# Two small constant loads issued by ScalarE instead of SyncE, in a two-block transformer kernel

## The chip, the cores and the metric

The kernel runs on 1 core of one Trainium2 chip. The metric is device time in microseconds (us): the median of several runs, and beside it one execution recorded by the hardware profiler. PE is TensorE's matmul, PEld its weight load, DVE is VectorE, ACT is ScalarE, POOL is GpSimd, SP is SyncE; "DMA" is the core's 16 transfer engines, which all work on each of the large transfers named here.

## The reference, cut to what matters

Two transformer blocks run one after the other on 512 tokens of width 1024, in float32. The first block is modulated by a conditioning vector `c`; only its first lines touch the place of the change:

```
c_act = silu(c)                                   # c is [1, 1024]
mod = c_act @ ada_w + ada_b                       # [1, 6*1024]: sh1, sc1, ga1, sh2, sc2, ga2
h = rmsnorm(x, pre_mix_g) * (1.0 + sc1) + sh1     # x is [512, 1024]
proj = h @ w_in                                   # convolution input (glu), q, k, v, gates
...
x = x + ga1 * rmsnorm(mixer(proj), post_mix_g)
x = x + ga2 * rmsnorm(swiglu_ffn(...), post_ffn_g)
x = second_block(x)                               # retention, MLA attention, convolutional FFN
```

So the first matrix product, `h @ w_in`, needs three things: the norm of `x`, the scale and shift `sc1` and `sh1` that come from `silu(c)` and 2 of the 6 parts of `ada_w`, and the weights.

## The kernel before, in words

Everything is stored transposed: 1024 features are 8 chunks of 128 partitions, and the 512 tokens lie along the free dimension. Each engine runs its own written-out program, one after another, and they meet at semaphores. Every float32 product is made of three products of split operands (`_hi` and `_lo`). Work goes in stages of weight groups (`STAGES`), and the first stage is `glu`, whose 8 chunks (`glu_chunk`, L761) each need one chunk of `h_hi` and `h_lo`.

The start of the program has four strands.

**Transfers.** SP issues all of them, from one queue, in the order in which its program is written: `small` (128 x 24 numbers, among them `c` as a column per chunk and the constant eps), `ident` (the 128 x 128 identity), four parts of `x` (512 KB each), `vec` (the vectors), two tiles of `ada_w` for chunk 0 (`load_first(0)`, L463, 512 KB each), half a weight group of glu (`glu_half(0)`, L468, 512 KB). Then SP waits until the fourth part of `x` is in, and goes on with further tiles of `ada_w` and of glu weights.

**The conditioning row.** ACT loads its function table (L1360), waits for `small` and takes exp(-c) (L1362). DVE makes `silu(c)` out of it in three tiny steps (L2308 to L2312), waits for `ident`, and spreads the 1024 values along diagonals (`c_spread`, L2315). PE multiplies that by a matrix of ones (L733), and so has the whole row of `silu(c)` on every partition, and DVE copies it out of PSUM into `c_row` (L2321). `c_columns`, the function with L2308 to L2315, is the first thing in DVE's program after two memsets, and the copy stands after the second of DVE's four `add_pair` steps:

```
c_columns()
for quarter in range(4):
    add_pair(quarter)
    if quarter == 1:
        c_copy()
dve.wait_ge(sem["in_vec"], 16)
dve.wait_ge(sem["c_act"], 8)
for c in range(DC):
    modulate(c)
```

**The norm.** ACT squares each part of `x` as it lands (L1366, `sq_first`), DVE adds pairs of chunks (`add_pair`, L2349), PE sums over partitions (L738), ACT takes the logarithm and the exponential (L1330, L1333) and so gets `rs`.

**The first chunk of h.** DVE multiplies a tile of `ada_w` by `c_row` and sums along it (`ada_column`, L2298), twice for a chunk: once for the scale, once for the shift. Then it makes `t_n` (L2274), and ACT adds the shift and rounds to `h_hi` (L1357), after it has rounded the first half of the weights to `w_hi` (L1372). PE's first matmul of the glu stage (L761) waits for both. Before that PE runs matmuls of a matrix of ones that nothing reads (L726, `warm`), and in its program the product with `c_spread` stands between the first 9 of them and the sums of L738.

Of the kernel before, what the change touches and what calls it, by code (L numbers as in the profile page):

```python
# [218 lines left out]
def build(nc, dram, out):  # L219
# [4 lines left out]
    def fixed(name, shape, dt=F32):  # L224
        size = int(np.prod(shape[1:])) * 4
        t = nc.alloc_sbuf_tensor_at(name, shape, dt, offset=off[0])
        off[0] += (size + 31) // 32 * 32
        return t
# [9 lines left out]
    vec, small = fixed("vec", [P, N_VEC]), fixed("small", [P, N_SMALL])  # L238
# [5 lines left out]
    ident, ones_r, block_mean = fixed("ident", [P, P]), fixed("ones", [P, P], F32R), fixed("block_mean", [P, P])  # L244
# [133 lines left out]
    with ExitStack() as ctx:  # L378
        sem = {n: ctx.enter_context(nc.semaphore(n)) for n in names}
# [67 lines left out]
        def _(sp):  # L447
# [25 lines left out]
                for r, buf in enumerate(bufs):  # L473
                    sp.dma_start(buf[:, :], dram["ada"][a + r]).then_inc(sem[done], 16)

            sp.dma_start(small[:, :], dram["small"]).then_inc(sem["in_small"], 16)
            sp.dma_start(ident[:, :], dram["mats"][:, 0, :]).then_inc(sem["in_ident"], 16)
            for part in range(4):
                two = slice(2 * part, 2 * part + 2)
                sp.dma_start(x[:, two, :], dram["x"][:, two, :]).then_inc(sem[f"x_ada{part}"], 16)  # L480
# [741 lines left out]
        def _(act):  # L1222
# [16 lines left out]
            def fold_highs(stage, k):  # L1239

                name, slot, n = stage.name, k % 2, fold_nth[stage.name, k]
                ext_hi, _, ext_f = fold_ext(stage)
                act.wait_ge(raw_full[slot], 16 * (stage.g0 // 2 + k // 2 + 1))
                again = k - 2 >= FOLDS[name]
                if again:
                    act.wait_ge(sem["fold_mm"], mm_count[name, k - 2, 2])
                else:
                    act.wait_ge(sem["tile_done"], 2 * (stage.g0 + k) - 2)
                yield A(block_of(w_hi[slot], LEFT), block_of(raw[slot], LEFT), ACT.Copy).then_inc(sem["fold_hi"], 1)
                act.wait_ge(sem["fold_sum"], 4 * n + 3)  # L1250
                if again:
                    act.wait_ge(sem["fold_mm"], mm_count[name, k - 2, 5])
                yield A(ext_hi[slot][:, :, :, :], ext_f[slot][:, :, :, :], ACT.Copy).then_inc(sem["fold_hi"], 1)
                act.wait_ge(sem["fold_sum"], 4 * n + 4)
                if again:
                    act.wait_ge(sem["tile_done"], 2 * (stage.g0 + k) - 2)
                yield A(block_of(w_hi[slot], RIGHT), block_of(raw[slot], RIGHT), ACT.Copy).then_inc(sem["w_hi_done"], 1)
# [99 lines left out]
                    A(dst, src[:, :], ACT.Identity, bias=shift).then_inc(sem["made_hi"], 1)  # L1357


            nc.scalar.preload_act_table_set("natural_log_exp_and_others")  # L1360
            act.wait_ge(sem["in_small"], 16)
            A(row_stat[:, 0, 0:DC], small[:, SMALL["c"]:SMALL["c"] + DC], ACT.Exp, scale=-1.0).then_inc(sem["c_act"], 1)  # L1362
# [565 lines left out]
            def ret_pair(stage, i0):  # L1928
                def evac(_, slot, k, ahead):
                    i = i0 + k  # L1930
                    for s in range(2):
                        n = 2 * i + s
                        if s == 1 and i < PAIRS - 1:
                            act.wait_ge(sem["z_done"], HEADS + n + 1)
                            stage_q(i + 1, rqk)
                        act.wait_ge(sem["sp_done"], 2 * HEADS + n + 1)
                        A(t_hi[:, :], rp[:, :], ACT.Copy).then_inc(sem["sph_done"], 1)
                        if s == 0:
                            ahead()
                        elif i < PAIRS - 1:  # L1940
                            stage_qk(i + 1, rqk, rkey_dup, begun=True)
                        if n < 4:
                            decays(n + 4)
                        else:
                            beside_scores(n)
                        act.wait_ge(sem["ro_done"], n + 1)
                        A(rqk[head_rows(s), i, :], o_ps[0:HD, :], ACT.Copy).then_inc(sem["o_half"], 1)
                        if n >= 4:
                            beside_values(n)
                    if i < PAIRS - 1:  # L1950
                        act.wait_ge(sem["v_centred"], max(1, i + 1))
                        stage_v(i + 1, rv_rows, ret_v)
                return evac
# [195 lines left out]
        def _(dve):  # L2149
# [836 lines left out]

            def ret_pair(i0):
                def evac(_, slot, k, ahead):
                    i = i0 + k
                    for s in range(2):  # L2990
# [518 lines left out]
```

## Time and profile before

| | |
|---|---|
| median of 3 runs | 1330.96 us (1330.03 to 1331.42) |
| the profiled execution, its own time | 1328.96 us |
| its span, first to last instruction | 1327.10 us |
| PE matmul busy | 1309.0 us (99% of the span) |
| DVE busy | 1045.7 us (79%) |
| ACT busy | 731.6 us (55%) |
| first matmul of the glu stage starts | 16.04 us |

The times of the engines come from the profiled execution, whose own time is 1.86 us longer than the span between its first and last instruction. It is 2.00 us below the median of the runs shown, and 1.07 us below the lowest of them. Busy shares are averages over all stages. The first 16 us, before the glu stage starts, are another regime than the rest.

### The profile page before, as it was taken

The page shows a single profiled execution, that of the slowest core. Times are in us where ns is not written, and L with a number is a line of the kernel's source. Part 1 is how long each engine was busy: PE and PEld are TensorE (multiplying, and loading weights), DVE is VectorE, ACT ScalarE, POOL GpSimd, SP SyncE. Part 2 cuts the span into 40 slices and gives each one's busy share as a digit, 9 for nine tenths or more (in the row PEclk, how much of TensorE's full clock was granted, in tenths as well). Part 3 has the DMA queues.
Part 4 walks back from the last instruction along what each step waited for, and adds up shares of the span by engine and source line. Part 5 has one row for each costly group of instructions (what it writes and reads, how often), then busy time and mean ns, then how long its engine had stood idle before and what let it go on. Part 6 is the DMA issues. An engine that isn't in the chain of part 4 may idle for free. (4 is left out here: it accounts for less than half of the span.)

```text
span 1327.1 us, 19480 instructions
## 1 busy us (share of the span) xinstructions
PE 1309.0 (99%) x7546; PEld 1150.7 (87%) x7546; DVE 1045.7 (79%) x1317; ACT 731.6 (55%) x1045; POOL 113.2 (9%) x86
## 2 busy tenths in 40 slices
PE   8999999999999999999999999999999999999997
PEld 6889888879989989989999897888888898889886
DVE  7899999999989689746849769997577876786663
ACT  4424888785546345534545856787365434443444
POOL 0000000012100591000012001010200000000001
PEclk9999999999999999999999999999999999999999
DMA  9634411167333433222252151301222232223212
GB/s 366 256 128 112 159 63 48 33 220 277 131 149 104 143 143 122 101 96 96 96 191 72 64 175 48 93 27 64 96 95 95 95 100 91 95 95 128 77 69 76
DMA packets 28731, 155.60 MB, mean 117 GB/s; under 512 B 3248, under 2 KB 5680, under 8 KB 15600
## 3 DMA queue, kind: packets, MB, share of 16 engines
q1 hardware_dynamic: 28656, 154.58, 33.4%
q8 instruction: 50, 0.82, 0.3%
q14 instruction: 25, 0.20, 0.0%
HBM read 145.39 MB, written 4.19 MB: 113 GB/s over the span
## 5 line engine op out<-in xcount | busy, mean ns | idle before, releaser
L2155 DVE TENSOR_TENSOR w_lo<-raw,w_hi 128x2048 fp32r<-128x2048 f32 (+3 forms) x139 | 249.4, 1796 | 47.0 <-ACT w_hi L1237 35.3
L1237 ACT ACTIVATE w_hi<-raw 128x2048 fp32r<-128x2048 f32 (+2 forms) x74 | 131.2, 1773 | 31.3 <-PE psum L920 15.4
L658 PE MATMUL psum<-h_hi,w_hi 128*128 128x512 f32 x360 | 92.1, 394 | 0.1
L658 PE MATMUL psum<-h_hi,w_lo 128*128 128x512 f32 x360 | 91.1, 391 | 0.0
L658 PE MATMUL psum<-h_lo,w_hi 128*128 128x512 f32 x360 | 90.4, 389 | 0.0
L658 PE MATMUL psum<-xg_hi,w_hi 128*128 128x512 f32 x336 | 83.0, 389 | 0.0
L658 PE MATMUL psum<-xg_hi,w_lo 128*128 128x512 f32 x336 | 83.0, 389 | 0.0
L658 PE MATMUL psum<-xg_lo,w_hi 128*128 128x512 f32 x336 | 83.0, 389 | 0.0
L658 PEld LDWEIGHTS psum<-h_lo,w_hi 128*128 128x128 f32 x360 | 67.6, 188 | 14.1
L658 PEld LDWEIGHTS psum<-h_hi,w_lo 128*128 128x128 f32 x360 | 67.0, 188 | 13.7
L658 PEld LDWEIGHTS psum<-h_hi,w_hi 128*128 128x128 f32 x360 | 66.0, 188 | 14.2 <-DVE w_lo L2155 0.7
L3220 DVE TENSOR_TENSOR up_raw<-psum,rs 128x512 f32<-128x512 f32 x44 | 30.2, 687 | 56.5 <-PE psum L658 54.2
L658 PEld LDWEIGHTS psum<-xg_lo,w_hi 128*128 128x128 f32 x336 | 63.1, 188 | 13.1
L658 PEld LDWEIGHTS psum<-xg_hi,w_lo 128*128 128x128 f32 x336 | 63.1, 188 | 13.1
L658 PEld LDWEIGHTS psum<-xg_hi,w_hi 128*128 128x128 f32 x336 | 62.9, 188 | 13.0
L3360 POOL COPY sq_sum<-sq 128x256 f32<-128x256 f32 (+1 forms) x6 | 3.6, 608 | 622.3 <-ACT sq L1323 622.3
L2091 ACT ACTIVATE up_a<-up_raw,vec 128x512 f32<-128x512 f32 x22 | 18.0, 816 | 58.5 <-DVE up_raw L3220 58.5
L2091 ACT ACTIVATE up_b<-up_raw,vec 128x512 f32<-128x512 f32 x22 | 17.9, 816 | 53.9 <-DVE up_raw L3220 53.9
L920 PE MATMUL psum<-h_hi,w_hi 128*128 128x256 f32 x288 | 46.5, 284 | 0.3 <-DVE act_p L2712 0.2
L2437 DVE SCALAR_TENSOR_TENSOR conv_tmp<-u,vec,conv_tmp 128x512 f32<-128x512 f32 x62 | 46.7, 753 | 0.0
L920 PE MATMUL psum<-h_lo,w_hi 128*128 128x256 f32 x288 | 46.3, 283 | 0.0
L920 PE MATMUL psum<-h_hi,w_lo 128*128 128x256 f32 x288 | 46.3, 283 | 0.0
(501 smaller groups left out, 3336.7 us busy)
## 6 DMA issues: line engine op xcount, KB each, us to landing
raw<-w_ffn_in SPq DMA_DIRECT2D x22, 1024.0 KB, 4.9
raw<-w_up SPq DMA_DIRECT2D x22, 1024.0 KB, 4.8
ada_first<-ada SPq DMA_DIRECT2D x16, 512.0 KB, 12.0
raw<-w_gate SPq DMA_DIRECT2D x8, 1024.0 KB, 4.9
raw<-w_mix_out SPq DMA_DIRECT2D x8, 1024.0 KB, 4.9
raw<-w_ffn_out SPq DMA_DIRECT2D x8, 1024.0 KB, 4.9
raw<-w_down SPq DMA_DIRECT2D x8, 1024.0 KB, 4.8
ada_x<-ada SPq DMA_DIRECT2D x11, 512.0 KB, 5.3
```

The lines of the kernel that those rows point to most:

```text
L658: last = mm(ps, w[slot][:, k, t * P:(t + 1) * P], part(xv, k0 + k), start=first, stop=final)
L920: last = mm(into, w[a][:, k, :], xv[b][:, k, :], start=(p in (1, 7) and a == b and k == 0), stop=(b == 1 and k == 3), skip_group_check=True)
L1237: A(w_hi[slot][:, 0:stage.kc, :], raw[slot][:, 0:stage.kc, :], ACT.Copy).then_inc(sem["w_hi_done"], 1)
L2091: A(buf[:, :], up_raw[t][s][:, :], ACT.Identity, scale=col("conv_w_2", 2 * 2 * FC + t * FC + chan), bias=col("conv_b_2", t * FC + chan)).t ...
L2155: return tt(out_lo, full, high.bitcast(F32), ALU.subtract)
L2437: stt(u[:, c, PAD:PAD + S] if last else sums[a][:, :], u[:, c, bass.ds(j, S)], col("conv_w", c * TAPS + j), sums[a][:, :], ALU.mult, ALU.a ...
L3220: by_rs = lambda: tt(up_raw[t][s][:, :], bank[2 * s + t], rs[:, :], ALU.mult)
L3360: last = nc.gpsimd.tensor_copy(sq_sum[:, cols], sq[q % 2][:, cols])
```

## The change

The transfers of `small` and `ident` leave SP's program, where they were its first two, and become the first two things that ACT issues, ahead of the load of its function table. Neither what is moved nor who waits for it is changed. All names and line numbers in the text are those of the kernel before, except in rows that are marked as the changed kernel's.

```diff
@@ block.sync
-            sp.dma_start(small[:, :], dram["small"]).then_inc(sem["in_small"], 16)
-            sp.dma_start(ident[:, :], dram["mats"][:, 0, :]).then_inc(sem["in_ident"], 16)
             for part in range(4):
                 two = slice(2 * part, 2 * part + 2)
                 sp.dma_start(x[:, two, :], dram["x"][:, two, :]).then_inc(sem[f"x_ada{part}"], 16)
@@ block.scalar
+            act.dma_start(small[:, :], dram["small"]).then_inc(sem["in_small"], 16)
+            act.dma_start(ident[:, :], dram["mats"][:, 0, :]).then_inc(sem["in_ident"], 16)
             nc.scalar.preload_act_table_set("natural_log_exp_and_others")
             act.wait_ge(sem["in_small"], 16)
             A(row_stat[:, 0, 0:DC], small[:, SMALL["c"]:SMALL["c"] + DC], ACT.Exp, scale=-1.0).then_inc(sem["c_act"], 1)
```

SP's queue begins like this, before (-) and after (+); a DMA row stands for one transfer (or for as many as the number at its end), and the line numbers after L475 sink by two.

```order
-L476 DMA small<-small 128x24
-L477 DMA ident<-mats 128x128
-L480 DMA x<-x 128x1024 x4
-L481 DMA vec<-vec 128x427
+L478 DMA x<-x 128x1024 x4
+L479 DMA vec<-vec 128x427
 L463 DMA ada_first<-ada 128x1024 x2
 L468 DMA raw_52<-w_glu 128x1024
```

The four parts of `x`, and everything behind them, have moved two places forward. ACT's program begins like this, again with - before and + after; `row_stat` is the place of exp(-c), `sq_first` that of the squares.

```order
-L1221 UNCONDITIONAL_BRANCH
+L1219 UNCONDITIONAL_BRANCH
+L1358 DMA small<-small 128x24
+L1359 DMA ident<-mats 128x128
 L1360 ACT_TABLE_LOAD
 L1362 ACTIVATE row_stat<-small 128x8
 L1366 ACTIVATE sq_first_71<-x 128x1024 x2
 L1366 ACTIVATE sq_first_72<-x 128x1024 x2
```

The table load, and with it the exponential of `c`, has moved two places back. The programs of PE, DVE and POOL are the same in both kernels.

## Rows read from the trace of the kernel before

**Rows 1.** The page: the span, and busy time, share and instructions of two engines.

```profile
span 1327.1 us, 19480 instructions
PE 1309.0 (99%) x7546; PEld 1150.7 (87%) x7546; DVE 1045.7 (79%) x1317; ACT 731.6 (55%) x1045; POOL 113.2 (9%) x86
```

**Rows 2.** Stretches after 16 us: length, busy of five engines, PEclk, DMA share, GB/s.

```profile
16.00:60.00 44.00, 43.97 (x191) 35.63 (x192) 39.02 (x57) 16.18 (x16) 0.00 (x0) 1.00 0.75 294
60.00:1327.10 1267.10, 1252.70 (x7305) 1106.89 (x7303) 996.89 (x1244) 706.75 (x1020) 113.03 (x82) 1.00 0.32 109
```

**Rows 3.** Timeline of PE from 0 to 28 us: start, us, instruction, idle before.

```profile
4.78 1.90 PE L733 MATMUL psum<-c_spread,ones 128*128 128x512 f32 x4
...
10.65 1.98 PE L738 MATMUL psum<-sq_first,ones 128*128 128x512 f32 x4 [0.61 <-DVE sq_first L2349]
...
16.04 2.12 PE L761 MATMUL psum<-h_hi,w_hi 128*128 128x512 f32 x8 [0.94 <-ACT h_hi L1357]
```

**Rows 4.** Timeline of ACT from 0 to 16 us.

```profile
0.73 1.28 ACT L1360 ACT_TABLE_LOAD   x1 [0.73 <-PEq L3502]
2.46 0.21 ACT L1362 ACTIVATE row_stat<-small 128x8 f32<-128x8 f32 x1 [0.44 <-DMA small<-small]
5.81 1.06 ACT L1366 ACTIVATE sq_first<-x 128x1024 f32<-128x1024 f32 x1 [3.14 <-DMA x<-x]
7.09 1.06 ACT L1366 ACTIVATE sq_first<-x 128x1024 f32<-128x1024 f32 x1 [0.22 <-DMA x<-x]
...
9.62 1.06 ACT L1366 ACTIVATE sq_first<-x 128x1024 f32<-128x1024 f32 x1 [0.24 <-DMA x<-x]
12.74 0.69 ACT L1330 ACTIVATE ln_ms<-psum,small 128x512 f32<-128x512 f32 x1 [2.06 <-PE psum L738]
...
14.31 1.06 ACT L1372 ACTIVATE w_hi<-raw 128x1024 fp32r<-128x1024 f32 x1 [0.22 <-DMA raw<-w_glu]
15.28 0.71 ACT L1357 ACTIVATE h_hi<-t_n,mod 128x512 fp32r<-128x512 f32 x1
```

**Rows 5.** Timeline of DVE from 0 to 16 us.

```profile
3.42 1.22 DVE L2315 TENSOR_TENSOR c_spread<-ident,row_stat 128x1024 f32<-128x1024 f32 x1
...
8.79 1.22 DVE L2321 COPY c_row<-psum 128x1024 f32<-128x1024 f32 x1
9.92 1.49 DVE L2349 TENSOR_TENSOR sq_first<-sq_first 128x512 f32<-128x512 f32 x2
11.62 1.28 DVE L2298 CUSTOM_DVE_ANT_0 ada_first<-ada_first,c_row,vec 128x1024 f32<-128x1024 f32 x1 [0.22 <-DMA ada_first<-ada]
...
14.23 0.75 DVE L2274 SCALAR_TENSOR_TENSOR t_n<-x,gain,rs 128x512 f32<-128x512 f32 x1
```

**Rows 6.** Stretches up to 39 us, the same columns as rows 2.

```profile
0.00:1.70 1.70, 0.65 (x3) 0.65 (x4) 0.30 (x2) 0.97 (x1) 0.20 (x4) 1.00 0.00 0
1.70:2.20 0.50, 0.50 (x4) 0.50 (x4) 0.00 (x0) 0.31 (x1) 0.00 (x0) 1.00 0.19 25
2.20:2.72 0.52, 0.52 (x5) 0.52 (x4) 0.02 (x1) 0.21 (x1) 0.00 (x0) 1.00 0.39 111
...
5.00:9.60 4.60, 3.48 (x8) 0.97 (x6) 2.12 (x3) 3.17 (x3) 0.00 (x0) 1.00 1.03 385
...
16.00:39.00 23.00, 22.96 (x100) 18.73 (x101) 21.94 (x33) 7.69 (x7) 0.00 (x0) 1.00 1.02 415
```

**Rows 7.** Timeline of SP from 0 to 16 us (its DMA issues).

```profile
0.74 0.41 SPq L476 DMA_DIRECT2D small<-small  x1
1.20 0.42 SPq L477 DMA_DIRECT2D ident<-mats  x1
1.67 1.85 SPq L480 DMA_DIRECT2D x<-x  x4
```

**Rows 8.** DMA issues from 0 to 16 us: KB of each, us from issue to landing.

```profile
ident<-mats SPq DMA_DIRECT2D x1, 64.0 KB, 2.0
small<-small SPq DMA_DIRECT2D x1, 12.0 KB, 1.7
```

## The prediction

> **What bounds the kernel now.** I read the page first: PE works 1309.0 of 1327.1 us [rows 1]. Then the stretches after the glu stage has begun: PE is busy 43.97 of 44.00 us up to 60, and 1252.70 of 1267.10 us (98.9%) from there to the end [rows 2]. The waits that stand there are for work of other engines, none for a point in time. So whatever moves the first glu matmul, at 16.04 us [rows 3], moves the end by as much, and the change can be judged in the first 16 us.
>
> There I followed the timelines back from that matmul. It waits for `h_hi`, which ACT starts at 15.28, right after `w_hi`, which started at 14.31 on the landing of the glu weights [rows 4]. DVE's `t_n` at 14.23 stands right behind two `ada_column` steps, the first of which started at 11.62 on the landing of a tile of `ada_w` [rows 5]. The norm's squares start at 5.81, 7.09 and (the last) 9.62, each on the landing of a part of `x` [rows 4]. Three strands, and each waits for a transfer. The stretches say why: from 5.00 to 9.60 all 16 DMA engines are busy (share 1.03, 385 GB/s), and from 16 to 39 still (1.02) [rows 6]. The start is bound by one stream of bytes, in SP's order, and by the moment at which that stream comes up to speed.
>
> The fourth strand, the conditioning row, has time to spare. From the start of `c_spread` the chain to `h_hi` is: `c_spread` 1.22, then 0.14 until PE begins L733 and 1.90 for it [rows 3, 5], 0.11 for the handover (as from the end of L738, 10.65 + 1.98, to L1330 at 12.74) [rows 3, 4], 1.13 from the copy to the next `add_pair` (8.79 to 9.92), 1.49 for two of these, 2.61 for two `ada_column` steps (11.62 to 14.23), and 1.05 from `t_n` to `h_hi` (14.23 to 15.28) [rows 4, 5]. The sum is 9.65 us. With `c_spread` at 3.42 the strand alone would allow `h_hi` at 13.07; its slack is 2.21 us.
>
> **The change part by part.** *Removed from SP:* two issues ahead of `x`. Their starts and that of `x` are 0.74, 1.20 and 1.67 [rows 7], so `x`, and everything behind it on SP, is issued 1.67 - 0.74 = 0.93 us earlier. SP's next wait, for the fourth part of `x`, ends as much earlier as that part lands.
>
> *The bytes of the two stay.* Before, they moved while nothing else did: the DMA share is 0.00 up to 1.70, then 0.19 for 0.50 us and 0.39 for 0.52 us [rows 6], which is 0.10 + 0.20 = 0.30 us of all 16 engines, and 12.5 + 58 = 70 KB of their 76 KB. From 0.74 to the first bytes is about 1 us, so `x` (issued 1.67) came at about 2.7, and will now come at about 1.8. In the new kernel the two loads move beside `x`, and take their 0.30 us out of a stream that is the bound. The gain of the stream is 0.93 - 0.30 = **0.63 us**. Its upper end is 0.93, if the two fill gaps while the stream comes up to speed.
>
> *Added to ACT:* two issues. At SP's spacing of 0.46 us each, the table load begins at 0.73 + 0.93 = 1.66 and ends 1.28 later at 2.94 [rows 4, 7]; the exponential then starts at about 2.96 instead of 2.46. That wait was for `small`, so half a microsecond of the ACT time is new delay. `c_spread` comes 0.96 after the exponential (2.46 to 3.42) [rows 4, 5], so at 3.92. To keep the gain of 0.63, `h_hi` must start at 14.65, and `c_spread` by 14.65 - 9.65 = 5.00. The cover is still 1.08 us; I cost the delay at nothing. Behind the exponential on ACT stand the four squares; the first can start when the first part of `x` lands, now at 5.81 - 0.93 = 4.88 or later, so they don't wait for it either.
>
> The Trainium skill, "ScalarE: Activation LUTs", section "What ACT_TABLE_LOAD costs", speaks against that: it puts a drain of 1.38 us behind each load. No such drain stands in this trace, where the load ends at 2.01 and the exponential, at 2.46, waited for `small` [rows 4]. By the page the exponential would start at 4.3 and `c_spread` at 5.3, which would take back an estimated 0.3 us of the gain.
>
> *Landing of the two beside `x`.* No row here has two issuing queues at work at once, so this is bounded from both sides. At best they land as before, 1.7 and 2.0 us after issue [rows 8], at 2.44 and 3.20. If every row of theirs (128 over 16 engines, 8 for each engine and load) takes a turn behind a 4 KB row of `x`, which at 385 GB/s over 16 engines lasts 0.17 us, then 8 turns are 1.4 us: `small` lands at about 3.8 and `c_spread` could start at 4.8; `ident`, 16 turns behind the start at 1.7 and 0.4 us for its landing (before: bytes moved by about 2.8, landed 3.2), at 4.9. Both are just under 5.00. At worst they stand behind `x` itself; that is a rival.
>
> *The sum:* 0.63 us from the stream, nothing given back: the profiled execution of 1328.96 us would become 1328.33, and its span of 1327.10 would become 1326.47. That execution lies 2.00 us below the median shown, and I take the same step from the median: 1330.96 - 0.6 = **1330.4 us**.
>
> **The rivals.** *Issues take turns (1330.8).* If one queue's issue keeps the other's from being worked on, `x` starts behind one of ACT's two, at 1.20 instead of 0.74, and the gain is 0.63 - 0.46 = 0.17 us. The table load would then end at 0.73 + 1.86 + 1.28 = 3.87 and `c_spread` come at 4.83, which is still hidden. Against it: an issue takes 0.41 us for 12 KB and 0.42 for 64 KB [rows 7], so most of it looks like the issuing engine's own work. The Trainium skill, "Perfetto Trace Analysis", section "DMA Instruction — HWDGE (DVE, Sync)", has it that the descriptor generator is shared and locked for exclusive use; by that page the turns would happen. No row here can show it.
>
> *The two stand behind the first parts of x (1331.5).* If `small` lands with the first part, at 4.88, and `ident` with the second, at 7.09 - 0.93 = 6.16, then `c_spread` starts at 6.16 and `h_hi` at 15.81: 0.53 us later than now, and the slack has become the bound.
>
> *They stand behind all of x (1335.0, slower).* Then `small` lands with the last part, at 9.62 - 0.93 = 8.69, `c_spread` comes at 9.65 and `h_hi` at 19.30: 4.02 us later, and PE idles that long ahead of the glu stage. The price grows one for one from a `c_spread` at 5.63 (no change); it passes 0.2% (2.66 us) when `small` lands after 7.33. For it: `x` has all engines for itself from its first bytes on, and is 2 MB against 76 KB. Against it: the loads are issued beside the first part, not behind the fourth.
>
> The Trainium skill, "DMA: Bandwidth & Descriptors", section "Queues, rings and completion order", says that each transfer engine goes round its queues, one packet at a time. By that page neither of the last two rivals happens; no row here shows it, and their chances stand.
>
> **How the numbers follow.** Forecast (gain of 0.2 to 0.9, 1330.0 to 1330.8): 0.62. Turns: 0.15. Behind the first parts: 0.13. Behind all of `x`: 0.05. What I see nothing of, above all the 1.86 us of the time that lie outside the span, in which a second queue might cost or save something: 0.05, split 0.03 faster and 0.02 slower. A measurement of this kernel can tell about 0.2%, 2.66 us, from no change; no mechanism here gains that, since the two issues are worth 0.93 at most. So faster is 0.03, slower 0.05 + 0.02 = 0.07, within 0.2% is 0.90. The range takes the forecast, the turns and the first parts (1330.0 to 1331.5) and the scatter of the runs shown, about 0.7 us to either side: 1329.3 to 1332.2.
>
> **What would show it.** Right: the first issue of `x` at 0.74; the first square near 5.2; the exponential near 3.0 to 3.8; `c_spread` before 5.0 and not the last to arrive; the first glu matmul near 15.4; the stretches from there on as before. Wrong: an issue on ACT much longer than 0.46; a first square that moves less than 0.2; DVE idle ahead of `c_spread` on `ident`, and after 5.6; a first glu matmul that moves and an end that doesn't, which would mean that something after 16 us was tied to another clock than PE's.

## The result, and the profile after

| | before | after |
|---|---|---|
| median of 12 runs each | 1330.26 us (1328.26 to 1331.84) | 1332.33 us (1330.19 to 1334.28) |
| ratio, after to before | | 1.0017 (1.0010 to 1.0025) |
| the profiled execution's own time | 1328.96 us | 1330.23 us |
| its span | 1327.1 us | 1328.1 us |
| first glu matmul in it | 16.04 us | 16.06 us |

The changed kernel is slower, by 0.17%: 1332.33 - 1330.26 = 2.07 us, and the interval (1.3 to 3.3 us) excludes zero. That is 0.13 us above the range, and the forecast gain of 0.6 us isn't there. The profiled execution is one of the quickest of the twelve (the lowest took 1330.19), so by itself it shows only a part of the loss.

SP's timeline of the changed kernel (start, us, instruction) shows the step that was meant: `x` is issued at 0.74 instead of 1.67 [rows 7], and its four issues take 1.91 us instead of 1.85.

```profile
0.74 1.91 SPq L478 DMA_DIRECT2D x<-x  x4
```

ACT's timeline of the same execution, with the idle time before an instruction in brackets, answers to [rows 4].

```profile
0.73 0.41 ACTq L1358 DMA_DIRECT2D small<-small  x1
1.17 0.45 ACTq L1359 DMA_DIRECT2D ident<-mats  x1
1.66 1.28 ACT L1360 ACT_TABLE_LOAD   x1 [1.66 <-PEq L3502]
4.17 0.21 ACT L1362 ACTIVATE row_stat<-small 128x8 f32<-128x8 f32 x1 [1.23 <-DMA small<-small]
4.80 1.06 ACT L1366 ACTIVATE sq_first<-x 128x1024 f32<-128x1024 f32 x1 [0.43 <-DMA x<-x]
...
8.84 1.06 ACT L1366 ACTIVATE sq_first<-x 128x1024 f32<-128x1024 f32 x1 [0.23 <-DMA x<-x]
13.06 0.69 ACT L1328 ACTIVATE ln_ms<-psum,small 128x512 f32<-128x512 f32 x1 [3.16 <-PE psum L736]
...
15.29 0.72 ACT L1355 ACTIVATE h_hi<-t_n,mod 128x512 fp32r<-128x512 f32 x1
```

The stream gained what was forecast and a little more: the first square starts 5.81 - 4.80 = 1.01 us earlier, the last 9.62 - 8.84 = 0.78. But `h_hi` starts at 15.29, as before (15.28). In between, the exponential waited 1.23 us for `small` after the table load. DVE's timeline, which answers to [rows 5], shows the other load late as well:

```profile
5.79 1.22 DVE L2315 TENSOR_TENSOR c_spread<-ident,row_stat 128x1024 f32<-128x1024 f32 x1 [0.77 <-DMA ident<-mats]
...
9.09 1.23 DVE L2321 COPY c_row<-psum 128x1024 f32<-128x1024 f32 x1 [0.87 <-PE psum L731]
10.23 1.28 DVE L2349 TENSOR_TENSOR sq_first<-sq_first 128x512 f32<-128x512 f32 x2
...
14.44 0.75 DVE L2274 SCALAR_TENSOR_TENSOR t_n<-x,gain,rs 128x512 f32<-128x512 f32 x1 [0.32 <-ACT rs L1331]
```

`c_spread` waits for `ident` and starts at 5.79 instead of 3.42. From there the delay goes on by way of the norm: the copy of `c_row` waits for PE and stands in DVE's program ahead of the last two `add_pair` steps (10.23), PE's norm sums come behind these, `ln_ms` starts at 13.06 instead of 12.74 [rows 4], and `t_n` waits last for `rs`, 0.32 us. The view of the DMA issues (KB of each, us from issue to landing) has 3.4 us for `small` and 4.6 for `ident` where [rows 8] have 1.7 and 2.0; the second profile of the kernel before has 1.6 and 3.1, so `ident` scatters there too:

```profile
ident<-mats ACTq DMA_DIRECT2D x1, 64.0 KB, 4.6
small<-small ACTq DMA_DIRECT2D x1, 12.0 KB, 3.4
```

PE's timeline, which answers to [rows 3], shows what this leaves: from the end of the first warm matmuls to the product with `c_spread`, PE idles 1.81 us.

```profile
1.06 4.21 PE L724 MATMUL psum<-ones 128*128 128x128 f32 x18 [1.06 <-DVE ones L2301]
7.07 1.98 PE L731 MATMUL psum<-c_spread,ones 128*128 128x512 f32 x4 [1.81 <-DVE c_spread L2315]
...
16.06 1.20 PE L759 MATMUL psum<-h_hi,w_hi 128*128 128x512 f32 x4 [0.65 <-ACT h_hi L1355]
```

From 16 us on, the stretches are those of [rows 2], except that the last is 1.00 us longer while PE's busy time there grew by 0.31:

```profile
16.00:60.00 44.00, 43.94 (x191) 35.62 (x192) 39.00 (x57) 16.18 (x17) 0.00 (x0) 1.00 0.73 286
60.00:1328.10 1268.10, 1253.01 (x7305) 1107.08 (x7303) 998.41 (x1244) 706.75 (x1020) 113.15 (x82) 1.00 0.32 109
```

### The profile page after: what moved, and what is told of

Its sections match the earlier page's. It is cut to its first block and busy times, and to the rows that moved or that the text cites. A ratio compares the mean times of both kernels' runs of the same rounds, so it can differ in the third digit from the quotient of the medians.

```text
span 1328.1 us, 19480 instructions
## 1 busy us (share of the span) xinstructions
PE 1309.3 (99%) x7546; PEld 1151.3 (87%) x7546; DVE 1047.0 (79%) x1317; ACT 731.6 (55%) x1045; POOL 113.3 (9%) x86
```

## The experiments

Three theories stood at the start: the two loads land too late, and what hangs on the late row costs the time; a second queue costs time by itself, wherever its loads land; or nothing is lost ahead of 16 us, and later waits differ from one execution to the next. All kernels of a batch ran on one chip, beside runs of the kernel before. Lines shift by one to three between the kernels, so the product with `c_spread` is L731 to L734.

**Both kernels again.** Their programs are unchanged.

> The kernel before once more, as a measure of how far two sets of runs of one kernel lie apart, and for a second trace of it. All theories: ratio 1.000, within 0.001 to either side; first glu matmul at 16.0 us. The theory that the remaining 1 to 2 us are scatter of the later waits for the copies inside SBUF (qkT at about 112 us, rqk at about 771 us) expects these waits of ACT (3.3 and 3.9 us in the first trace) to differ by up to some tenths from trace to trace, and the span with them.

> The changed kernel once more. Strand theory (the two loads move beside x, land late, and the conditioning row takes what x gained): c_spread again at 5.6 to 6.0 us, first glu matmul at 16.0 to 16.1, no further place in the program where the change costs anything; ratio 1.000 to 1.001. Queue theory (a second queue in use costs 1 to 2 us behind the first matmul): ratio 1.001 to 1.0025 again, with a first glu matmul near 16.06, and the same later places longer than in both traces of the kernel before. Scatter theory: the later waits (3.9 and 4.4 us in the first trace of the changed kernel) are different this time.

Measured: the kernel before 1330.1 us, ratio to its other runs 1.0003 (0.9994 to 1.0012); the changed kernel 1331.43 us, 1.0015 (1.0006 to 1.0024). So the loss repeats. The second profile of the changed kernel was worth more than the first: its first glu matmul stands at 17.34 instead of 16.06. PE's timeline of it:

```profile
7.12 3.00 PE L731 MATMUL psum<-c_spread,ones 128*128 128x512 f32 x4 [2.15 <-DVE c_spread L2315]
9.91 4.32 PE L736 MATMUL psum<-sq_first,ones 128*128 128x512 f32 x8
...
17.34 0.96 PE L759 MATMUL psum<-h_hi,w_hi 128*128 128x512 f32 x3 [0.65 <-ACT h_hi L1355]
```

`c_spread` started at 5.84 there, as in the first profile (5.79). What differs is that the product took 3.00 us instead of 1.98. The stretches of this execution (length, busy time of PE, PEld, DVE, ACT and POOL, PEclk, DMA share, GB/s) show why:

```profile
5.00:7.00 2.00, 0.00 (x0) 0.00 (x0) 1.23 (x3) 1.59 (x2) 0.00 (x0) 1.00 1.02 398
7.00:8.00 1.00, 0.88 (x2) 0.49 (x3) 1.00 (x3) 0.79 (x2) 0.00 (x0) 0.98 1.04 424
8.00:9.00 1.00, 1.00 (x2) 0.33 (x1) 0.27 (x1) 0.78 (x2) 0.00 (x0) 0.50 1.04 401
9.00:11.00 2.00, 2.00 (x4) 0.90 (x3) 0.84 (x1) 0.92 (x1) 0.00 (x0) 0.50 1.03 416
11.00:12.00 1.00, 1.00 (x3) 0.29 (x2) 1.00 (x3) 0.00 (x0) 0.00 (x0) 0.82 1.04 418
```

PE did nothing from 5 to 7 us, and behind that idle time the granted clock fell to 0.50 (1.2 of 2.4 GHz): it was 0.50 from 8 to 11 us and for part of the next microsecond. The four matmuls of the product and those of the norm sums ran through it, and the whole start came 17.34 - 16.06 = 1.28 us later. The runs list a mean granted clock each: it is 0.996 or 0.997 in 16 of the 23 runs of the changed kernel, and 0.998 or 0.999 in the other 7. Of the 92 runs of the kernel before in these batches (81 beside the other kernels and the 11 of its own set) 2 are as low. The 16 have a median of 1331.8 us; four of the 7 lie at 1330.0 to 1330.3, the other three at 1333.2 to 1333.8, for which I have no trace.

**One load each on ACT.** Either kernel moves half of the change:

```diff
# ident_act: SP keeps small
-            sp.dma_start(ident[:, :], dram["mats"][:, 0, :]).then_inc(sem["in_ident"], 16)
+            act.dma_start(ident[:, :], dram["mats"][:, 0, :]).then_inc(sem["in_ident"], 16)
             nc.scalar.preload_act_table_set("natural_log_exp_and_others")
# small_act: SP keeps ident
-            sp.dma_start(small[:, :], dram["small"]).then_inc(sem["in_small"], 16)
+            act.dma_start(small[:, :], dram["small"]).then_inc(sem["in_small"], 16)
             nc.scalar.preload_act_table_set("natural_log_exp_and_others")
```

> Half of the change: only the identity goes to ACT's queue, the small constants stay first on SP's. Strand theory: small lands near 2.5 as before, ident (issued at 0.73, ahead of the first bytes of x at about 2.2) lands by 4.0, c_spread starts before 4.3 and is hidden again, x is issued 0.46 us earlier, and the first glu matmul starts at 15.5 to 15.8; ratio 0.9996 to 0.9999. Queue theory: first matmul as early, and the time still 1 to 2 us above before (ratio 1.001 to 1.002).

> The other half: only the small constants go to ACT's queue, the identity stays first on SP's. Strand theory: ident (issued 0.74) and small (0.73) both move before the first bytes of x come at about 2.2, both land by 3.0; table load at 1.2 to 2.5, c_spread before 4.0 and hidden; first glu matmul at 15.5 to 15.8, ratio 0.9996 to 0.9999. If small still lands after 3.8, the delay comes from ACT's queue and not from x. Queue theory: ratio 1.001 to 1.002 with the matmul as early.

> The small constants on ACT's queue, the identity first on SP's, once more, as the version that did best. Strand and clock theory: c_spread before 4.0, no gap of PE over 1 us, first glu matmul at 15.5 to 15.9, mean granted clock 0.998 to 0.999 in all runs, ratio 0.999 to 0.9998. Queue theory: over 1.000.

> The identity alone on ACT's queue, once more, to narrow the interval of the version with one load on each queue. Strand and clock theory: first glu matmul at 15.5 to 15.9, mean granted clock 0.998 or 0.999 in all runs, ratio 0.9992 to 0.9999.

Measured: `ident` alone 1328.83 us, 0.9995 (0.9986 to 1.0004), and again 1329.74, 0.9997 (0.9988 to 1.0006); `small` alone 1328.74 us, 0.9993 (0.9984 to 1.0002), and again 1329.41, 0.9996 (0.9987 to 1.0005). No run of the 44 has a low mean clock. Both use the second queue, and neither is slower, so the theory that this queue costs time by itself fell. The rows of `small_act` show what is different; PE's timeline, ACT's, and the DMA issues:

```profile
4.93 1.98 PE L732 MATMUL psum<-c_spread,ones 128*128 128x512 f32 x4
...
15.53 2.11 PE L760 MATMUL psum<-h_hi,w_hi 128*128 128x512 f32 x8 [0.90 <-ACT h_hi L1356]
```

```profile
1.17 1.28 ACT L1360 ACT_TABLE_LOAD   x1 [1.17 <-PEq L3502]
2.69 0.21 ACT L1362 ACTIVATE row_stat<-small 128x8 f32<-128x8 f32 x1 [0.24 <-DMA small<-small]
```

```profile
ident<-mats SPq DMA_DIRECT2D x1, 64.0 KB, 2.1
small<-small ACTq DMA_DIRECT2D x1, 12.0 KB, 1.9
```

With one load ahead of `x` and one beside it, `x` is issued half as much earlier, both land about 2 us after their issue, PE goes from the warm matmuls into the product without a gap, and the first glu matmul comes at 15.53, 0.51 us before that of [rows 3] (15.67 in the second profile of `small_act`; 15.86, a little later than expected, and 15.56 in those of `ident_act`).

**The gap, filled in the changed kernel and opened in the one before.** Now the theory was that the clock's price hangs on PE's idle time. The first of these kernels takes more warm matmuls before the product; the second has the loads on SP as before, but lets PE wait for the second part of `x` ahead of the product; the third does both.

```diff
# after_warm14, on the changed kernel
-WARM = (9, 0, 0, 0, 11)
+WARM = (14, 0, 0, 0, 11)
# before_gap, on the kernel before, ahead of the product with c_spread (L733)
+                    pe.wait_ge(sem["x_ada1"], 16)
# before_gap_warm14: both edits on the kernel before
```

> The changed kernel with 14 instead of 9 matmuls of ones ahead of the product with c_spread; nothing else. Clock theory (the late c_spread leaves PE idle for about 2 us, and in most executions the granted clock then falls to half for some us, which delays the first glu matmul by about 1.3 us more): PE idles about 1 us or less ahead of L731, the clock stays at 1.00 in the stretches from 7 to 12 us, the first glu matmul starts at 16.0 to 16.1, the mean granted clock of a run is 0.998 or 0.999 in nearly all runs, and the ratio to the kernel before is 0.9995 to 1.0005. Strand theory alone (the late conditioning row, without the clock) expects the same ratio as for the changed kernel, since c_spread is as late. Queue theory: 1.001 to 1.002.

> The kernel before, with both loads on SP's queue, in which PE waits for the second part of x ahead of the product with c_spread (L733); nothing else. Clock theory: PE idles for about 2.1 us (4.9 to 7.1) as in the changed kernel; where the clock holds, the first glu matmul is at 16.0 to 16.2; in about two of three runs the mean granted clock is 0.996 or 0.997 instead of 0.998, and the ratio is 1.0008 to 1.002. Queue theory: only one queue is in use, so the ratio is 1.000 to 1.0003. Strand theory alone: at most 0.3 us later (the copy of c_row at 9.1 instead of 8.8), ratio 1.000 to 1.0003.

> The kernel before with PE's added wait for the second part of x ahead of L733, and with 14 instead of 9 matmuls of ones ahead of that wait. Clock theory: the wait is still there, but PE idles only about 1 us, the product with c_spread takes 1.9 to 2.0 us again instead of 3.4, the first glu matmul is at 16.0 to 16.2, and the ratio 0.9995 to 1.0004. If the wait itself (the later copy of c_row) made the loss of the run without the added matmuls, the ratio stays at 1.0008 to 1.002 and the first glu matmul at 17 or more.

Measured:

| kernel | median us | ratio to before | first glu matmul |
|---|---|---|---|
| changed, gap filled | 1329.99 | 1.0000 (0.9991 to 1.0009) | 16.08 |
| before, gap opened | 1331.15 | 1.0012 (1.0003 to 1.0021) | 17.50 |
| before, gap opened and filled | 1328.65 | 0.9995 (0.9986 to 1.0004) | 16.30 |

PE's timeline of the changed kernel with the gap filled:

```profile
1.05 5.29 PE L724 MATMUL psum<-ones 128*128 128x128 f32 x28 [1.05 <-DVE ones L2301]
7.08 1.98 PE L731 MATMUL psum<-c_spread,ones 128*128 128x512 f32 x4 [0.74 <-DVE c_spread L2315]
```

The product starts at 7.08, as in the changed kernel, since `c_spread` is as late (5.80); but the gap is 0.74 us, none of the 11 runs has a low mean clock, and the loss is gone, with both loads still on the second queue. PE's timeline of the kernel before with the gap opened, and under it the product's matmuls (ns, lowest/median/highest):

```profile
7.09 3.40 PE L734 MATMUL psum<-c_spread,ones 128*128 128x512 f32 x4 [1.83 <-DMA x<-x]
...
17.50 0.73 PE L762 MATMUL psum<-h_hi,w_hi 128*128 128x512 f32 x2 [0.65 <-ACT h_hi L1358]
```

```profile
L734 PE MATMUL psum<-c_spread,ones x4: 714/1061/1190, 7.1 to 9.8; 128*128 128x512 f32 x4
```

Here `c_spread` was ready early (its step starts at 3.47), one queue issues everything, and PE's gap alone gives the late start: matmuls of up to 1190 ns, where the product of [rows 3] is four in 1.90 us. With the gap filled as well:

```profile
7.34 1.95 PE L734 MATMUL psum<-c_spread,ones 128*128 128x512 f32 x4 [0.38 <-DMA x<-x]
...
16.30 0.97 PE L762 MATMUL psum<-h_hi,w_hi 128*128 128x512 f32 x3 [0.66 <-ACT h_hi L1358]
```

It starts later than without the filling (7.34 against 7.09) and yet the first glu matmul comes 17.50 - 16.30 = 1.20 us earlier (at 16.30, 0.1 us later than expected).

Two things didn't go with the theory as it stood: only 3 of the 11 runs with the gap opened have a low mean clock, and the clock column of its profile reads 1.00 from 7 to 11 us, over the matmuls of 1190 ns. The traces explain the column, and in part the mean. Their clock records do not begin with the program. In every trace the warm matmuls behind the very first take 421 ns each, and from where the first clock record begins a warm matmul takes 275 ns and one of the product about 592. Ahead of it the column reads 1.00 because no record stands there, and the mean counts that time as full: the profiled run with the gap opened has a mean of 0.999. That first rise comes at 4.54 us in the second profile of the changed kernel, at 5.33 in its first, and at 10.02, in the midst of the product, in the kernel with the gap opened; the other eight traces have it between 4.05 and 7.29. The first 18 warm matmuls show it (ns, lowest/median/highest), in the second profile of the changed kernel and under it with the gap opened:

```profile
L724 PE MATMUL psum<-ones x18: 274/421/582, 1.1 to 4.7; 128*128 128x128 f32 x18
L726 PE MATMUL psum<-ones x18: 421/421/580, 1.1 to 4.8; 128*128 128x128 f32 x18
```

So in the first of these the clock had risen; it fell again at 7.95, behind the idle time. In the second it had not risen yet, and no warm matmul was fast; PE then stood idle, and the product itself ran slow. Either way the product comes behind a gap and runs at the low level. In the first profile of the changed kernel it rose at 5.33, just behind its last warm matmul, and the product ran fast in spite of the gap of 1.81 us. With the gap filled, the clock had risen ahead of the product in both kernels (at 5.07 and 6.35) and stayed. Each of these is one execution; that the gap and not chance decides rests on the timed runs, 1.0012 with it opened and 0.9995 with it filled.

**Later waits.** Waits for copies inside SBUF, far behind the start, scatter between executions. For the same copy, the view of waits of the changed kernel has 3.9 us in its first profile and 2.5 in its second:

```profile
ACT pair L1435 <- DMA qkT<-qkT: 3.9, 1, 3.9
```

```profile
ACT pair L1435 <- DMA qkT<-qkT: 2.5, 1, 2.5
```

So single spans move by about a microsecond whatever the start did: the spans of the two profiles of the changed kernel are both 1328.1 us, although their first glu matmuls are 1.28 apart, and the second profile of the kernel before has 1328.1 as well, with its first glu matmul at 15.96. The kernel before has 3.3 and 4.3 there in its two profiles. The theory that nothing but this scatter is there fell with the timed runs: the loss came back in the second set of the changed kernel and went with the gap.

## Why the prediction was wrong

**What held.** The view of the bound: the start is one stream of bytes, and it came up 0.78 to 1.01 us earlier for the 0.63 to 0.93 forecast. ACT's side: table load at 1.66, as worked out, and its end at 2.94. The length of the rest of the conditioning strand: 15.29 - 5.79 = 9.50 us from `c_spread` to `h_hi`, for 9.65. Here the number is in part luck, since the last wait is not the one in the sum. I had the strand end in the two `ada_column` steps; they were done by 14.12, and `t_n` began at 14.44, when `rs` was there. The late row had gone through the copy of `c_row` into the last two `add_pair` steps and so into the norm, which the sum has as a strand of its own. The rival of issues that take turns did not happen: `x` is issued at 0.74 beside ACT's issue at 0.73. The Trainium skill, "Perfetto Trace Analysis", section "DMA Instruction — HWDGE (DVE, Sync)", has a descriptor generator that DVE's and SP's sequencers share and lock; it does not speak of ACT, as the prediction took it to, and no such wait between SP and ACT stands in these rows. Nor does the drain that the Trainium skill, "ScalarE: Activation LUTs", section "What ACT_TABLE_LOAD costs", adds to a table load: with `small` early, in `small_act`, the exponential came 0.24 us after the load, and waited for `small`.

**The step that failed** is the landing of the two beside `x`, "both just under 5.00". It was mis-sized: `small` was there at about 4.13 (0.73 + 3.4, forecast 3.8) and `ident` at 5.77 (1.17 + 4.6, forecast 4.9), so `c_spread` came at 5.79 and not by 5.00, between the forecast and the rival behind the first parts (6.16). The late 0.79 us took back the whole gain of the stream, and the slack of 2.21 us became a wait. The loads did move beside `x` and not behind it, as the DMA queues' packets, MB and share of 16 engines from 2.10 to 3.55 us show (q1 is SP's queue, q10 ACT's):

```profile
q1 hardware_dynamic: 89, 0.36, 69.3%
q10 hardware_dynamic: 74, 0.01, 6.9%
```

Both queues are served, 89 packets to 74. The Trainium skill, "DMA: Bandwidth & Descriptors", section "Queues, rings and completion order", has each engine go round its queues, one packet at a time; the counts agree in that neither queue waits for the other's end, but how many rows one turn has they don't show. What I had wrong is the size. I took 0.17 us for a turn from the full stream, and here the stream was not yet full (69.3% and 6.9% of the engines' time), so that a row of `x` passed each engine only every 1.45 x 16 / 89 = 0.26 us. And I took all engines for the mean one, while a load has landed only with its last row. ACT's queue from 3.55 to 4.55 us, when `ident` moves, and under it from 4.55 to 5.30:

```profile
q10 hardware_dynamic: 142, 0.06, 22.3%
q10 hardware_dynamic: 7, 0.00, 1.3%
```

Nearly all of its packets were through by 4.55, and 7 stragglers held the landing until 5.77. Why these came last is open. The prediction's own count was loose as well: `small` is worked out as its earliest landing plus 8 turns (2.44 + 1.4), `ident` as 1.7 + 16 x 0.17 + 0.4, which makes 4.8 and not 4.9; worked out like `small` it would be 3.20 + 2.7 = 5.9, past the bound. I had put the results, 4.8 and 4.9, against a bound of 5.00, and called a margin of 0.1 us a cover.

**The term that was missing** is the clock. I followed the late strand to `h_hi` and not to PE, whose warm matmuls end at about 5 us and whose next work hangs on `c_spread`. In the sum a late `c_spread` cost one for one from 5.63 on. By the runs it also opens a gap of 1.8 to 2.2 us in PE's work, and in most executions (16 of 23 by the mean clock) the clock is then at 1.2 GHz under the product and the norm sums. That is worth 17.34 - 16.06 = 1.28 us between two executions of the changed kernel, and 17.50 - 16.30 = 1.20 between the kernels with the gap opened and filled. Filling the gap took the changed kernel from 1.0015 to 1.0000, opening it took the kernel before to 1.0012, without any of the change. The Trainium skill, "TensorE: Matmul & The Clock Gate", Part 1, has the low level as the default, which work ends and idling brings back. These runs agree with the direction: 421 ns for the first warm matmuls and 275 for later ones, and a fall behind 2.15 us of idle time.

So the sum by the runs is: gain of the stream 0.8, taken back by the landing 0.8, clock 1.2 to 1.3 in most executions. That makes a loss of some 1.3 us, at the lower end of the interval of the result (1.3 to 3.3) and inside that of the repeat (0.06% to 0.24%, 0.8 to 3.2 us). Whether something more stands behind the 2.07 us of the first set is open; so is why the clock falls in some executions and not in others. The three runs of 1333.2 to 1333.8 with a high mean clock may be such in which the first rise came late, which the mean does not count; no trace of them shows it.

**The better version** is half of the change, either half. The four sets average 0.9995 (0.9993, 0.9995, 0.9996, 0.9997), a gain of about 0.6 us that agrees with a first glu matmul 0.2 to 0.5 us earlier; but each interval holds 1.000, so I call it likely and not shown.

## What to carry to other kernels

Here a small load that moved beside a large one on another queue shared the engines with it and landed late (4.6 us after issue instead of 2.0 or 3.1); one that moved while nothing else had bytes to move, in the first microsecond after the large one's issue, landed about 2 us after its own. So move as many loads as fit there, not all that can be moved. And when a product comes late, follow it to PE and ask how long PE idles, and whether its clock has risen by then: the idle time can cost a stretch at half clock on top, and here matmuls that nothing reads, enough to cover most of the new gap, took that back. In the first microseconds read the clock from the durations of matmuls of one shape, since the clock column reads 1.00 where it has no record.

## What was not expected of the hardware

An idle time of 2.15 us on PE, early in the program, was followed by a granted clock of 0.50 from 8 to 11 us, and this, not the late load by itself, is the price of the change. The moment of the clock's first rise scatters: between 4.05 and 7.29 us in ten traces, and 10.02 with the gap opened. So the kernel before can have slow matmuls there too: in its second profile the first rise is at 7.29, and the product took 2.80 us instead of 1.90, after an idle time of only 0.34 us, but `c_spread` was early enough (4.33) that the first glu matmul stayed at 15.96. The clock column read 1.00 over matmuls that took 714 to 1190 ns in the kernel with the gap opened, where [rows 3] have four in 1.90 us, because the trace's first clock record begins only in the last of them.
